# Softmax attention in a hybrid decoder: projections, norms and rotation with tokens on partitions, then transposes

## The chip, the cores and the metric

One core of a Trainium2 chip runs the whole program. The metric is the device time of one launch in microseconds (us). The engines are TensorE (PE), VectorE (DVE), ScalarE (ACT), GpSimd (POOL) and SyncE (SP), which issues most of the DMAs.

## What is computed

Two decoder layers over 256 tokens of width 1024, all in float32. Each layer runs three token mixers on the normed input (softmax attention, gated linear attention, causal pooling), gates and merges them, projects and adds; then a feed-forward part follows, dense in layer 0, the best 2 of 8 experts in layer 1. The change touches the attention branch alone, up to its scores:

```python
def mla_branch(c_q, c_kv, k_rope, positions, g_cq, w_uq, g_ckv, w_ukv, g_qk_q, g_qk_k):
    q = (rms_norm(c_q, g_cq) @ w_uq).reshape(B, S, 8, 96)
    kv = (rms_norm(c_kv, g_ckv) @ w_ukv).reshape(B, S, 8, 64 + 64)
    k_nope, v = kv[..., :64], kv[..., 64:]
    k = concatenate([k_nope, k_rope for every head], axis=-1)      # 64 + 32
    q, k = rms_norm(q, g_qk_q), rms_norm(k, g_qk_k)                # over 96 features
    q, k = (concatenate([z[..., :64], rope(z[..., 64:], positions)], axis=-1) for z in (q, k))
    o = causal_block_attention(q, k, v)
```

`c_q` and `c_kv` have 256 features, `k_rope` 32; all three are columns of one projection of the normed input. `rope` turns the last 32 features of each head by an angle that depends on the token.

## The kernel before

Every engine has its program written out by hand, and semaphores order them. The 1024-wide products run in pieces. A weight block of about 1 MB (256 to 288 columns; one of the names in `LOADS`, such as `cq`, `ckv`, `gq`, `gk`, `oga`, `ogb`, `ua`, `ub`, `g0`) is loaded by SP into one of four ring slots, in the order of `LOADS`. ACT rounds a piece of it (a quarter) to `m_hi` (line 1265), DVE takes the rest `m_lo` (line 1696), and PE multiplies three times: high by high, high by low, low by high (`by_pieces`, line 565). There are four piece buffers, so ACT can round piece p of the next block as soon as PE has used piece p of this one. In `split(L, name, FIRST)` the first three pieces are done, in `split(L, name, LAST)` the fourth; other work of ACT and DVE stands between, in a fixed order.

PSUM: six banks are handed out in turn to the names in `MIX_USES`. A use waits until the use six places ahead of it has been freed. In layer 0 two more uses, `par` and `inv`, stand after the fifth; so `lr` (the second product out of the block `vb`) gets the bank of `va`, which DVE frees by a copy to `gvt` (line 1706) after it has split all of `vb`.

In each layer, from `cq` on, PE does in this order: `cq`, `ckv` with `kr` (the rope part again as a product of its own, 96 columns wide of which 32 count), `gq`, the sums of squares of both latents by a matrix of ones (`sslat`, line 642), `gk`, the query projection `q0` to `q3` (line 528), `oga`, the key projection `k0` to `k3` (line 528) and the value projection `vm0`, `vm1` (line 672), `ogb`, the sums of squares of all queries and keys as 32 products with one column of ones (`ssq`, line 684), the decay gate `z` (line 692), the rotation of the shared rope key by a fixed matrix (`rk`, line 699) and of the queries (`rq0` to `rq3`, line 704), `ua`, the inverse norms of the keys spread over features (`ssk0` to `ssk3`, line 713), `ub`, and then the gate block `g0` with which the scores begin. Queries and keys lie with features on partitions and 256 tokens along the free axis throughout. The plain float32 products (lines 528, 672, 684, 692, 704, 713) issue two matmul instructions each; a transpose issues one.

ACT squares and copies each bank (lines 1327 to 1381) and takes the roots. DVE inverts the latent roots in a 128x512 tile (line 1653), scales the latents (line 1733), copies the values (line 1754), turns the queries (lines 1784 and 1787; POOL multiplies by the cosine, line 1163) and multiplies the keys by their inverse norms (line 1819). Between them DVE and ACT do the decay gate: DVE line 1777, ACT exponential and logarithm (lines 1376 and 1378), DVE lines 1792 and 1793. `tables()` (lines 1628 to 1648) makes sines and cosines once, in layer 0.

## Time and profile before

| | |
|---|---|
| median of 3 runs | 1252.97 us (1252.05 to 1253.17) |
| span of the profiled execution | 1251.2 us |
| PE / DVE / ACT / POOL busy | 94% / 68% / 54% / 7% |
| layer 0, from the start of `cq` to the start of `g0` | 41.3 to 129.5 us |
| layer 1, the same stretch | 515.9 to 604.1 us |
| experts, about | 790 us to the end |

The profiled execution has no time of its own beside its span, which leaves out what lies before the first and after the last instruction: the median stands 1.8 us above it. PE is "busy" from the start of a matmul to its modelled end, and these overlap; what a group of matmuls costs PE is read from the start of one group to the start of the next, and the chain of work gives exactly this.

### The profile page before, as it was taken

Reading aid. Unit: us, or ns where it says so; the run is one execution under the profiler, and the core shown is the slowest. Engines: PE = TensorE matmul, PEld = TensorE weight load, DVE = VectorE, ACT = ScalarE, POOL = GpSimd, SP = SyncE. Lnnn points to the kernel's source line nnn. Section 1 sums busy time; section 2 is a strip of 40 time slices with the busy share of each in tenths; the row PEclk is TensorE's granted clock in tenths of the full one; section 3 lists DMA queues with packets and bytes.
Section 4 is the critical chain, followed back from the end, with each engine's and each line's share of the span. In section 5 each row is a group of like instructions: output and inputs, shape, how many; then the busy total and the mean of one; then the engine's idle time right before and its main releaser. Section 6 shows DMA issues by size and latency. Waiting matters only on the chain.

```text
span 1251.2 us, 17893 instructions
## 1 busy us (share of the span) xinstructions
PE 1171.3 (94%) x6973; PEld 999.6 (80%) x6973; DVE 849.2 (68%) x1090; ACT 680.6 (54%) x922; POOL 88.7 (7%) x149
## 2 busy tenths in 40 slices
PE   3999899988999998999989988799999999999997
PEld 3978777877999998987867776787878888787885
DVE  3366877685545546445877686488888888888786
ACT  3464564544434434464464545376666666676664
POOL 5001412000000000001332000000000000000000
PEclk9998999998999999998989998799999999999999
DMA  6432343537537534242234447189989898988983
GB/s 195 161 104 102 107 139 132 168 121 266 186 124 247 185 134 160 93 136 101 80 123 148 165 135 269 53 306 332 306 297 324 288 341 288 337 302 306 316 303 121
DMA packets 146852, 250.17 MB, mean 200 GB/s; under 512 B 4318, under 2 KB 107860, under 8 KB 146772
## 3 DMA queue, kind: packets, MB, share of 16 engines
q1 hardware_dynamic: 144944, 246.82, 58.0%
q10 hardware_dynamic: 1828, 2.23, 0.6%
q8 instruction: 57, 0.93, 0.3%
q14 instruction: 23, 0.19, 0.1%
HBM read 247.98 MB, written 1.05 MB: 199 GB/s over the span
## 4 chain that ended last, share of the span: by engine, by line
PE 80%; DVE 10%; ACT 4%; issue 3%; POOL 1%; DMA 0%; ACTq 0%; DVEq 0%; POOLq 0%
PE PS L565 23%; PE PS L1047 9%; PE PS L1048 9%; PE PS L1049 9%; PE PS L910 5%; PE PS L912 5%; PE PS L911 5%; DVE m_lo L1696 3%; PE PS L1008 3%; PE PS L528 2%; ACT w_hi L339 2%; DVE w_lo L347 2%; PE PS L684 1%; PE PS L1019 1%; PE PS L591 1%
## 5 line engine op out<-in xcount | busy, mean ns | idle before, releaser
L347 DVE TENSOR_TENSOR w_lo<-ring,w_hi 128x1536 fp32r<-128x1536 f32 (+1 forms) x240 | 388.1, 1623 | 153.2 <-ACT w_hi L339 151.9
L339 ACT ACTIVATE w_hi<-ring 128x1536 fp32r<-128x1536 f32 (+1 forms) x240 | 329.3, 1378 | 160.3 <-PE PS L912 86.0
L1696 DVE TENSOR_TENSOR m_lo<-ring,m_hi 128x512 fp32r<-128x512 f32 (+2 forms) x256 | 185.8, 755 | 102.7 <-ACT m_hi L1265 101.3
L1265 ACT ACTIVATE m_hi<-ring 128x512 fp32r<-128x512 f32 (+2 forms) x256 | 157.6, 630 | 160.6 <-PE PS L565 158.8
L1047 PE MATMUL PS<-w_hi,hTe_hi 128*96 128x384 f32 (+1 forms) x512 | 169.9, 332 | 7.2 <-DVE w_lo L347 5.9
L1048 PE MATMUL PS<-w_hi,hTe_lo 128*96 128x384 f32 (+1 forms) x512 | 165.2, 323 | 0.0
L1049 PE MATMUL PS<-w_lo,hTe_hi 128*96 128x384 f32 (+1 forms) x512 | 165.0, 322 | 0.0
L565 PE MATMUL PS<-m_hi,h_hi 128*128 128x512 f32 (+1 forms) x288 | 108.3, 376 | 5.4 <-DVE gvt L1706 4.2
L565 PE MATMUL PS<-m_hi,h_lo 128*128 128x512 f32 (+1 forms) x288 | 103.3, 359 | 0.0
L565 PE MATMUL PS<-m_lo,h_hi 128*128 128x512 f32 (+1 forms) x288 | 103.0, 358 | 0.0
L910 PE MATMUL PS<-h_hi,w_hi 128*128 128x256 f32 x352 | 100.7, 286 | 0.7 <-DVE h_lo L1678 0.7
L912 PE MATMUL PS<-h_hi,w_lo 128*128 128x256 f32 x352 | 100.5, 286 | 0.0
L911 PE MATMUL PS<-h_lo,w_hi 128*128 128x256 f32 x352 | 100.5, 286 | 0.0
L1047 PEld LDWEIGHTS PS<-w_hi,hTe_hi 128*96 128x96 f32 x512 | 82.6, 161 | 17.8 <-issue 12.0
L1048 PEld LDWEIGHTS PS<-w_hi,hTe_lo 128*96 128x96 f32 x512 | 82.8, 162 | 7.3 <-issue 1.9
L1049 PEld LDWEIGHTS PS<-w_lo,hTe_hi 128*96 128x96 f32 x512 | 82.8, 162 | 5.0
L1047 PE MATMUL PS<-w_hi,hdT_hi 128*96 128x512 f32 x176 | 70.5, 400 | 0.9 <-issue 0.9
L910 PEld LDWEIGHTS PS<-h_hi,w_hi 128*128 128x128 f32 x352 | 68.6, 195 | 1.3 <-issue 1.1
L1048 PE MATMUL PS<-w_hi,hdT_lo 128*96 128x512 f32 x176 | 69.4, 394 | 0.0
L1049 PE MATMUL PS<-w_lo,hdT_hi 128*96 128x512 f32 x176 | 69.2, 393 | 0.0
L911 PEld LDWEIGHTS PS<-h_lo,w_hi 128*128 128x128 f32 x352 | 68.6, 195 | 0.2
L912 PEld LDWEIGHTS PS<-h_hi,w_lo 128*128 128x128 f32 x352 | 68.5, 195 | 0.0
(307 smaller groups left out, 2105.1 us busy)
## 6 DMA issues: line engine op xcount, KB each, us to landing
ring<-in_w_in_dram SPq DMA_DIRECT2D x40, 1024.0 KB, 5.1
ring<-in_w_exp_gate_dram SPq DMA_DIRECT2D x24, 1536.0 KB, 8.0
ring<-in_w_exp_up_dram SPq DMA_DIRECT2D x24, 1536.0 KB, 8.5
ring<-in_w_exp_down_dram SPq DMA_DIRECT2D x24, 1536.0 KB, 7.2
ring<-in_w_branch_dram SPq DMA_DIRECT2D x12, 1024.0 KB, 5.0
ring<-in_w_ffn_gate_dram SPq DMA_DIRECT2D x6, 1536.0 KB, 7.2
ring<-in_w_ffn_up_dram SPq DMA_DIRECT2D x6, 1536.0 KB, 7.1
ring<-in_w_ffn_down_dram SPq DMA_DIRECT2D x6, 1536.0 KB, 6.3
```

Of the source, the lines that this page charges most:

```text
L339: act.activation(w_hi[:, b, 0:words], ring[:, i % NSLOT, w0:w0 + words], ACT.Copy)\
L347: dve.tensor_tensor(w_lo[:, b, 0:words], ring[:, (j // 2) % NSLOT, w0:w0 + words], w_hi[:, b, 0:words].bitcast(F32), SUB).then_inc(sem(f"l ...
L565: mm = pe.matmul(dst, l, r, start=(kt == 0 and x == 0 and y == 0), stop=(kt == total - 1 and y == 2), skip_group_check=True)
L910: pe.matmul(dst, whi, xhi, start=start, stop=False, skip_group_check=True)
L911: pe.matmul(dst, whi, xlo, start=False, stop=False, skip_group_check=True)
L912: return pe.matmul(dst, wlo, xhi, start=False, stop=stop, skip_group_check=True)
L1008: mm = pe.matmul(PS[:, 4 + b, i * CAP:(i + 1) * CAP], htok[:, a, (4 * c + i) * P:(4 * c + i + 1) * P], psel[:, a, e, :], start=(a == 0), s ...
L1047: pe.matmul(dst, xhi, whi, start=start, stop=False)
L1048: pe.matmul(dst, xlo, whi, start=False, stop=False)
L1049: return pe.matmul(dst, xhi, wlo, start=False, stop=stop)
L1265: act.activation(hi, raw, ACT.Copy).then_inc(sem("m_hi_ready"), 1)
L1696: dve.tensor_tensor(lo, raw, hi.bitcast(F32), SUB).then_inc(sem("m_lo_ready"), 1)
```

## The change

Tokens lie on partitions for the attention projections. `cq` and `ckv` are computed by token block; `ckv` gives latent and rope key in one product of 288 columns. ACT takes the latents' sums of squares with an accumulator, DVE inverts four columns; both scale the latents, PE transposes them (`lt0`, `lt1`), and the gains are applied on the way out. Queries and keys with values come in four banks each (`QUADS`: token block, half of the heads). Their sums of squares are DVE reductions. The queries are turned and the keys scaled with tokens on partitions, and PE transposes both (`tq`, `tk`). Rope gains are multiplied into the sine and cosine tables (`rope_factors`, layer 0). Gone are `sslat`, `kr`, `vm`, `ssq`, `rk`, `rq`, `ssk`, `inv` and POOL's cosine products. Six small DMAs are added on SP's queue, one from ACT's queue is gone.

```diff
-MIX_USES = (["hm00", "hm01", "va", "hm10", "hm11", "vb", "lr", "cq", "ckv", "kr", "gq", "sslat", "gk"]
-            + [f"q{i}" for i in range(4)] + ["oga"] + [f"k{i}" for i in range(4)] + ["vm0", "vm1", "ogb", "ssq", "z", "rk"]
-            + [f"rq{i}" for i in range(4)] + ["ua"] + [f"ssk{i}" for i in range(4)] + ["ub"]
+QUADS = [f"{a}{hf}" for a in range(TT) for hf in range(2)]
+MIX_USES = (["hm00", "hm01", "va", "hm10", "hm11", "vb", "lr", "cq", "ckv0", "ckv1", "gq", "lt0", "lt1", "gk"]
+            + [f"q{x}" for x in QUADS] + ["oga"] + [f"kv{x}" for x in QUADS] + ["ogb", "z"]
+            + [f"tq{x}" for x in QUADS] + ["ua"] + [f"tk{x}" for x in QUADS] + ["ub"]
...
-USES[5:5] = [(-1, "par"), (-1, "inv")]
+USES[5:5] = [(-1, "par")]
@@ SP @@
+                if i == 2:
+                    for a in range(TT):
+                        sp.dma_start(posi[:, a:a + 1], A["positions"][:, a * P:(a + 1) * P].rearrange("b p -> p b"))\
+                          .then_inc(sem("pos_in"), 16)
+                    for x, g in enumerate(("g_qk_q", "g_qk_k")):
+                        for L in range(DEPTH):
+                            sp.dma_start(grope[:, x, L, :], A[g][L:L + 1, NOPE:QK].broadcast_to([P, ROPE]))\
+                              .then_inc(sem("grope_in"), 16)
@@ PE @@
+                by_pieces(L, "cq", [by_tokens(L, "cq")])
+                groups = []
+                for a in range(TT):
+                    bank, full = begin(L, f"ckv{a}")
+                    groups.append((full, [(bank[:, 0:RANK + ROPE], 0, RANK + ROPE, a)]))
+                by_pieces(L, "ckv", groups)
                 pair(L, "gq")
...
+                    bank, full = begin(L, f"lt{g}")
+                    for x in (("cq",), ("ckv0", "ckv1"))[g]:
+                        evacuated(L, x)
                     for i in range(KR):
-                        mm = pe.matmul(bank[:, g * T:(g + 1) * T], ones[:, :], sq[:, g * KR + i, :],
-                                       start=(i == 0), stop=(i == KR - 1))
-                mm.then_inc(full, 1)
+                        for a in range(TT):
+                            mm = pe.transpose(bank[:, i * T + a * P:i * T + (a + 1) * P],
+                                              latn[:, a, (g * KR + i) * P:(g * KR + i + 1) * P], ident[:, :])
+                    mm.then_inc(full, 1)
...
+                def from_latent(g, name, cols, w):
+
+                    for x in QUADS:
+                        a, hf = int(x[0]), int(x[1])
+                        bank, full = begin(L, f"{name}{x}")
+                        for i in range(KR):
+                            mm = pe.matmul(bank[:, 0:cols], latT[:, g * KR + i, a * P:(a + 1) * P],
+                                           w[:, i, hf * cols:(hf + 1) * cols], start=(i == 0), stop=(i == KR - 1))
+                        mm.then_inc(full, 1)
...
+                def heads(name, src, ready):
+
+                    for x in QUADS:
+                        a, hf = int(x[0]), int(x[1])
+                        bank, full = begin(L, f"{name}{x}")
+                        pe.wait_ge(sem(ready), L + 1)
+                        for i in range(4):
+                            mm = pe.transpose(bank[0:QK, i * P:(i + 1) * P], src[:, a, 4 * hf + i, :], ident[:, :])
+                        mm.then_inc(full, 1)
+
+                heads("tq", qt, "q_turned")
...
+                heads("tk", kt_, "k_scaled")
@@ ACT @@
+                split(L, "ckv", FIRST)
+                bank, _ = full(L, "cq")
+                for a in range(TT):
+                    act.activation(latsq[:, a, :], bank[:, a * RANK:(a + 1) * RANK], ACT.Square, accum_out=rl[:, a:a + 1])
+                split(L, "ckv", LAST)
+                split(L, "gq", FIRST)
+                for a in range(TT):
+                    bank, _ = full(L, f"ckv{a}")
+                    act.activation(latsq[:, 2 + a, :], bank[:, 0:RANK], ACT.Square, accum_out=rl[:, 2 + a:3 + a])\
+                       .then_inc(sem("latent_squares"), 1)
+                act.wait_ge(sem("latent_squares"), 2 * L + 2)
+                act.activation(rl[:, :], rl[:, :], ACT.Sqrt, bias=eps[:, 0:1], scale=1.0 / RANK).then_inc(sem("latent_roots"), 1)
+                for a in range(TT):
+                    bank, _ = full(L, f"ckv{a}")
+                    act.activation(krt[:, 1, a, :], bank[:, RANK:RANK + ROPE], ACT.Square, accum_out=sskr[:, a:a + 1])
+                    act.activation(krt[:, 0, a, :], bank[:, RANK:RANK + ROPE], ACT.Copy).then_inc(sem("kr_in"), 1)
+                act.wait_ge(sem("latent_inverse"), L + 1)
+                for a in range(TT):
+                    bank, free = full(L, f"ckv{a}")
+                    act.activation(latn[:, a, RANK:2 * RANK], bank[:, 0:RANK], ACT.Copy, scale=rl[:, 2 + a:3 + a]).then_inc(free, 1)
                 split(L, "gq", LAST)
+                split(L, "gk", FIRST)
+                bank, free = full(L, "lt0")
+                for i in range(KR):
+                    ins = act.activation(latT[:, i, :], bank[:, i * T:(i + 1) * T], ACT.Copy, scale=pcol("g_cq", L * KR + i))
+                ins.then_inc(free, 1)
+                split(L, "gk", LAST)
...
+                for x in QUADS:
+                    a, hf = int(x[0]), int(x[1])
+                    bank, _ = full(L, f"kv{x}")
+                    if hf == 0:
+                        act.wait_ge(sem("q_sums"), 2 * L + a + 1)
+                    kv = bank.rearrange("p (h c) -> p h c", h=4)
+                    n = 4 * NOPE
+                    act.activation(sqs[a][:, hf * n:(hf + 1) * n].rearrange("p (h c) -> p h c", h=4), kv[:, :, 0:NOPE], ACT.Square)
+                    act.activation(vt[:, a, hf * 4 * DV:(hf + 1) * 4 * DV].rearrange("p (h c) -> p h c", h=4), kv[:, :, NOPE:], ACT.Copy)\
+                       .then_inc(sem("kv_read"), 1)
+                act.activation(rq16[:, :], rq16[:, :], ACT.Sqrt, bias=eps[:, 1:2])
+                act.wait_ge(sem("k_sums"), L + 1)
+                act.activation(rk16[:, :], rk16[:, :], ACT.Sqrt, bias=eps[:, 0:1], scale=1.0 / QK).then_inc(sem("qk_roots"), 1)
                 split(L, "ua", FIRST)
                 out_gate(1)
                 split(L, "ua", LAST)
+                if L == 0:
+                    act.wait_ge(sem("gains_ready"), 1)
+                for x in QUADS:
+                    a, hf = int(x[0]), int(x[1])
+                    bank, free = full(L, f"tq{x}")
+                    act.activation(q[:, 4 * hf:4 * hf + 4, a * P:(a + 1) * P], bank[0:QK, :].rearrange("p (h t) -> p h t", h=4),
+                                   ACT.Copy, scale=pcol("g_qk_q", L, QK)).then_inc(free, 1)
 
                 act.wait_ge(sem("z_abs"), L + 1)
@@ DVE @@
+            def rope_factors():
+                dve.wait_ge(sem("rope_tables"), 1)
+                dve.wait_ge(sem("grope_in"), 16 * 2 * DEPTH)
+                cos, sin = (cs[:, i, :].rearrange("p (a j) -> p a j", a=TT) for i in range(2))
+                for L in range(DEPTH):
+                    for x in range(2):
+                        g = grope[:, x, L, :].rearrange("p (s j) -> p s j", s=2)
+                        by_cos, by_sin = (ropes[:, L, x, i, :, :].rearrange("p a (s j) -> p a s j", s=2) for i in range(2))
+                        for s in range(2):
+                            gs, other = (g[:, i, :].unsqueeze(1).broadcast_to([P, TT, HALF]) for i in (s, 1 - s))
+                            dve.tensor_tensor(by_cos[:, :, s, :], cos, gs, MUL)
+                            ins = dve.scalar_tensor_tensor(by_sin[:, :, s, :], sin, 1.0 if s else -1.0, other, MUL, MUL)
+                step(ins)
             def latent_inverse(L):
+                dve.wait_ge(sem("latent_roots"), L + 1)
+                dve.reciprocal(rl[:, :], rl[:, :]).then_inc(sem("latent_inverse"), 1)
+                dve.wait_ge(sem("latent_inverse"), L + 1)
+                bank, free = full(L, "cq")
+                for a in range(TT):
+                    ins = dve.tensor_scalar(latn[:, a, 0:RANK], bank[:, a * RANK:(a + 1) * RANK], rl[:, a:a + 1], None, MUL)
+                ins.then_inc(free, 1)
+            def turn_rope(x, tmp, by_cos, by_sin, last):
+                for s in range(2):
+                    ins = dve.tensor_tensor(tmp[..., s * HALF:(s + 1) * HALF], x[..., (1 - s) * HALF:(2 - s) * HALF],
+                                            by_sin[..., s * HALF:(s + 1) * HALF], MUL)
+                step(ins)
+                step(dve.tensor_tensor(x, x, by_cos, MUL))
+                last(dve.tensor_tensor(x, x, tmp, ADD))
...
+                split(L, "ckv"), split(L, "gq", FIRST)
+                latent_inverse(L)
+                split(L, "gq", LAST)
                 split(L, "gk", FIRST)
+                bank, free = full(L, "lt1")
+                for i in range(KR):
+                    ins = dve.tensor_scalar(latT[:, KR + i, :], bank[:, i * T:(i + 1) * T], pcol("g_ckv", L * KR + i), None, MUL)
+                ins.then_inc(free, 1)
...
                 split(L, "ogb", FIRST)
+                for a in range(TT):
+                    freed(L, f"q{a}1")
+                    dve.tensor_reduce(rq16[:, a * H:(a + 1) * H], sqs[a].rearrange("p (h c) -> p h c", h=H), AX.X, ADD)\
+                       .then_inc(sem("q_sums"), 1)
                 out_gate(0)
                 split(L, "ogb", LAST)
+                if L == 0:
+                    rope_factors()
+                by_cos, by_sin = (ropes[:, L, 1, i, :, :] for i in range(2))
+                dve.wait_ge(sem("kr_in"), 2 * L + 2)
+                turn_rope(krt[:, 0, :, :], krt[:, 1, :, :], by_cos, by_sin, step)
+                by_cos, by_sin = (ropes[:, L, 0, i, :, :].unsqueeze(2).broadcast_to([P, TT, H, ROPE]) for i in range(2))
+                turn_rope(qt[:, :, :, NOPE:QK], qtmp, by_cos, by_sin, lambda ins: ins.then_inc(sem("q_turned"), 1))
                 for a in range(TT):
+                    dve.wait_ge(sem("kv_read"), 4 * L + 2 * a + 2)
+                    step(dve.tensor_reduce(rk16[:, a * H:(a + 1) * H], sqs[a][:, 0:H * NOPE].rearrange("p (h c) -> p h c", h=H),
+                                           AX.X, ADD))
+                dve.tensor_tensor(rk16.rearrange("p (a h) -> p a h", a=TT), rk16.rearrange("p (a h) -> p a h", a=TT),
+                                  sskr.unsqueeze(2).broadcast_to([P, TT, H]), ADD).then_inc(sem("k_sums"), 1)
                 split(L, "ua", FIRST)
+                dve.wait_ge(sem("qk_roots"), L + 1)
+                step(dve.reciprocal(rqs[:, :], rq16[:, :]))
+                step(dve.reciprocal(rk16[:, :], rk16[:, :]))
+                for x in QUADS:
+                    a, hf = int(x[0]), int(x[1])
+                    bank, free = full(L, f"kv{x}")
+                    rk = rk16[:, a * H + 4 * hf:a * H + 4 * hf + 4].unsqueeze(2).broadcast_to([P, 4, NOPE])
+                    dve.tensor_tensor(kt_[:, a, 4 * hf:4 * hf + 4, 0:NOPE],
+                                      bank.rearrange("p (h c) -> p h c", h=4)[:, :, 0:NOPE], rk, MUL).then_inc(free, 1)
+                for a in range(TT):
+                    rk = rk16[:, a * H:(a + 1) * H].unsqueeze(2).broadcast_to([P, H, ROPE])
+                    ins = dve.tensor_tensor(kt_[:, a, :, NOPE:QK], krt[:, 0, a, :].unsqueeze(1).broadcast_to([P, H, ROPE]), rk, MUL)
+                ins.then_inc(sem("k_scaled"), 1)
                 out_gate(1)
                 split(L, "ua", LAST)
...
-                turned(2), turned(3)
-                split(L, "ub")
-                dve.wait_ge(sem("krope_read"), 2 * L + 2)
-                for i in range(4):
-                    bank, free = full(L, f"ssk{i}")
-                    x = k[:, 2 * i:2 * i + 2, :]
-                    dve.tensor_tensor(x, x, two(bank[0:QK, :]), MUL).then_inc(free, 1)
+                split(L, "ub", FIRST)
+                for x in QUADS:
+                    a, hf = int(x[0]), int(x[1])
+                    bank, free = full(L, f"tk{x}")
+                    dve.tensor_scalar(k[:, 4 * hf:4 * hf + 4, a * P:(a + 1) * P], bank[0:QK, :].rearrange("p (h t) -> p h t", h=4),
+                                      pcol("g_qk_k", L, QK), None, MUL).then_inc(free, 1)
+                split(L, "ub", LAST)
```

## Rows read from the trace of the kernel before

**Rows 1.** The page, busy time of each engine over the span.
```profile
PE 1171.3 (94%) x6973; PEld 999.6 (80%) x6973; DVE 849.2 (68%) x1090; ACT 680.6 (54%) x922; POOL 88.7 (7%) x149
```

**Rows 2.** Busy time by stretch: start:end, length, each engine, granted clock, DMA.
```profile
31.16:41.28 10.12, 10.12 (x72) 9.29 (x73) 2.58 (x4) 1.90 (x3) 0.00 (x0) 0.83 0.64 214
41.28:129.53 88.25, 88.25 (x601) 76.92 (x599) 52.12 (x88) 46.93 (x71) 5.73 (x4) 0.94 0.36 117
507.31:515.89 8.58, 8.58 (x74) 8.03 (x73) 4.79 (x8) 2.69 (x5) 0.00 (x0) 1.00 0.39 124
515.89:604.13 88.24, 88.24 (x600) 77.07 (x599) 45.47 (x66) 45.30 (x69) 5.80 (x4) 0.94 0.36 117
...
103.30:113.50 10.20, 10.20 (x29) 6.21 (x29) 5.13 (x10) 2.62 (x5) 2.39 (x2) 0.50 0.13 50
151.30:154.50 3.20, 0.38 (x6) 0.14 (x2) 2.96 (x10) 2.63 (x10) 2.95 (x5) 1.00 0.67 251
154.50:161.30 6.80, 6.35 (x20) 5.16 (x21) 6.49 (x15) 3.22 (x9) 5.52 (x7) 0.50 0.21 50
```

**Rows 3.** The chain of work in layer 0: start, length, engine and line.
```profile
21.32 0.54 PE PS L538 x4
...
27.82 2.63 DVE m_lo L1696 x4
30.45 0.61 DVE gvt L1706
...
31.16 30.34 PE PS L565 x240
61.50 1.73 PE PS L642 x8
63.22 5.75 PE PS L565 x48
68.97 6.91 PE PS L528 x32
...
81.63 7.05 PE PS L528 x32
88.68 3.63 PE PS L672 x8
...
98.06 8.57 PE PS L684 x64
...
108.63 6.05 PE PS L704 x8
...
120.44 3.49 PE PS L713 x32
...
137.43 0.43 DVE small L1833
```

**Rows 4.** Groups of DVE in layer 0, `cq` to `g0`, shapes apart.
```profile
L1653 DVE RECIPROCAL rt<-rt 128x512 f32<-128x512 f32 x1 | 3.4, 3353 | 1.1 <-ACT rt L1247 1.1
L1787 DVE TENSOR_TENSOR qk<-qk,th 32x512 f32<-32x512 f32 x4 | 3.2, 806 | 0.1
...
L1819 DVE TENSOR_TENSOR qk<-qk,PS 96x512 f32<-96x512 f32 x4 | 2.5, 679 | 0.0
L1777 DVE SCALAR_TENSOR_TENSOR scr<-scr 128x512 f32<-128x512 f32 x1 | 1.7, 1687 | 0.0
```

**Rows 5.** ACT in order of time, the decay gate of layer 0.
```profile
113.23 1.28 ACT L1378 ACT_TABLE_LOAD   x1
114.52 0.63 ACT L1378 ACTIVATE scr<-scr 128x512 f32<-128x512 f32 x1
```

**Rows 6.** DMA issues up to 140 us: engine, size, us to landing.
```profile
scr<-in_positions_dram ACTq DMA_DIRECT2D x1, 32.0 KB, 6.0
...
wr<-in_w_router_dram ACTq DMA_DIRECT2D x1, 32.0 KB, 9.5
```

**Rows 7.** Waits of SP's DMA queue: waited for, total, times, longest.
```profile
SPq L425 <- PE PS L616: 19.8, 1, 19.8
```

More of the change, by code:

```diff
@@ L252, in hybrid_trunk @@
         rk16 = small[:, 32:48]
+        rl, sskr = small[:, 28:32], small[:, 61:63]
         warmth = small[:, 60:61]
@@ L616, in parameters @@
                 pe.transpose(bank[:, 0:NPAR], ring[0:NPAR, NSLOT - 1, 0:P], ident[0:NPAR, 0:NPAR]).then_inc(full, 1)
-                bank, full = begin(-1, "inv")
-                pe.matmul(bank[0:QK, 0:1], invr[:, :], one1[:, :], start=True, stop=True).then_inc(full, 1)
             def mixer(L):
@@ L678, in mixer @@
-                evacuated(L, "q3")
-                evacuated(L, "k3")
-                for c, src in enumerate((sq, sk)):
-                    for a in range(TT):
-                        for h in range(H):
-                            x = c * TT * H + a * H + h
-                            mm = pe.matmul(bank[:, x:x + 1], src[0:QK, h, a * P:(a + 1) * P], ones[0:QK, 0:1],
-                                           start=True, stop=True)
-                mm.then_inc(full, 1)
+                evacuated(L, "lt1")
@@ L1240, in two @@
                 return ap.rearrange("p (a t) -> p a t", a=2)
-            def latent_root(L):
-                bank, free = full(L, "sslat")
-                if L:
-                    act.wait_ge(sem("latn_ready"), 4 * L)
-                act.activation(rt[:, :, :], two(bank), ACT.Sqrt, bias=eps[:, 0:1], scale=1.0 / RANK).then_inc(free, 1)
             warm = [0]
@@ L1316, in mixer @@
                     act.activation(par[:, :], bank[:, 0:NPAR], ACT.Copy).then_inc(free, 1)
-                    bank, free = full(-1, "inv")
-                    act.activation(invc[NOPE:QK, :], bank[NOPE:QK, 0:1], ACT.Copy).then_inc(free, 1)
+                    freed(-1, "par")
+                    c = PCOL["g_qk_q"]
+                    act.activation(par[NOPE:QK, c:c + 2 * DEPTH], ones[NOPE:QK, 0:2 * DEPTH], ACT.Copy).then_inc(sem("gains_ready"), 1)
                 split(L, "vb")
```

217 lines of the change are left out of this document (49 added, 168 removed).

## The prediction, made before the changed kernel ran

> **What bounds the kernel now.** I read the page first: PE is busy 94% of the span, DVE 68%, ACT 54% [rows 1]. Then I asked for busy time by stretch where the change acts, from the start of `cq` to the start of `g0`: 88.25 us in layer 0 and 88.24 us in layer 1, and in both PE has no idle time at all [rows 2]. DVE is busy 52.1 and 45.5 us there, ACT 46.9 and 45.3, so both have slack, but not so much that PE could shrink without end. Last I read the chain of work, which stays on PE from 31 us until the scores [rows 3]. What PE no longer does in this stretch should thus come off the time, less the waits that a faster PE runs into. The stretch is also at half clock in one place: 0.50, the lower level (1.2 GHz), from 103.3 to 113.5 us, after PE had done some 5 us of products with a single column [rows 2, 3].
>
> **PE's work in the stretch, rebuilt.** Prices per matmul instruction come from the chain [rows 3]. A float32r product of 256 columns is 5.75/48 = 0.12 us. A float32 one of 256 columns is 6.91/32 = 0.216 us, hence 0.324 for 384 and 0.43 for 512. A transpose is 0.54/4 = 0.135 us with the group's end in it; I take 0.12.
> - `cq`, `gq`, `gk`, `oga`, `ogb`, `ua`, `ub`, as before: 7 x 5.75 = 40.25.
> - `ckv` and `kr`: 72 instructions become 48 of 288 columns. No row has that width; at one column per cycle and the same fixed part 0.135 each, 6.45 (before 72 x 0.12 = 8.6). Bounds: 5.75 if width were free, 8.6 if nothing were won.
> - `sslat` (1.73) becomes 8 transposes, 1.0.
> - Queries: 32 x 256 columns become 16 x 384, 5.2 (before 6.91).
> - Keys and values: 7.05 + 3.63 = 10.7 become 16 x 512, 6.9.
> - `ssq`, 8.57, and `rk`, 0.4: nothing.
> - `z`: 1.6, what is left of the gap between the `ssq` and `rq` rows.
> - `rq`: 6.05 (at half clock; 8 x 0.43 = 3.4 at full) becomes 16 transposes, 1.9.
> - `ssk`: 3.49 becomes 16 transposes, 1.9.
>
> Sum 65.2 us, say 65.5 for the changes between kinds, against 88.25: 22.8 us less per layer. Nearly half is `ssq`, with the clock that it costs `rq`.
>
> **The clock.** Without one-column products, what can still pull it down is waiting or a run of transposes. The rows show a fall after a stretch in which PE was busy for 0.38 of 3.20 us: 0.50 for the following 6.8 us [rows 2]. The longest wait that I find below is 1.1 us; I take no new fall. The Trainium skill ("TensorE: Matmul & The Clock Gate", Part 4, PE-mode transpose) says that transposes do not count as activity for the clock gate in the way matmuls do. No transposes here stand alone for more than 1 us in a busy part, so no row settles it; that outcome is a rival below, priced from rows.
>
> **The start of layer 0.** `lr` takes the bank of `va` and waits for the copy to `gvt`, which ends at 31.1 us behind four low parts [rows 3]. With `inv` gone, `lr` gets the bank of `hm01`, long free, and PE begins `vb` when the first low part is there: 27.82 + 0.69 = 28.5 instead of 31.16, 2.65 us earlier. After the long wait `vb` ran at clock 0.83 and took 10.12 us; in layer 1, at 1.00, 8.58 [rows 2]. With a wait of under 2 us I expect full clock: 1.5 more. Together 4.2; bounds 2.65 and 4.2.
>
> **DVE and ACT.** DVE loses the 128x512 reciprocal 3.35, four scalings of latents (4 x 0.48), two copies of values (2 x 0.69), eight operations of turning (4 x 0.69 + 3.2), the key scaling 2.5 and three small ones of 0.42: about 16.3 us [rows 4]. It gains, at about 1 ns per column and 0.15 fixed (0.43 for a reduction over 256 columns [rows 3], 0.68 for 512): latents 1.9, query sums 2 x 0.95, turning of rope key and queries 0.8 + 2.4, key sums 2 x 0.69 + 0.2, key scaling 1.8 + 0.8, copies out of `tk` 2.5: 13.7. So DVE gets 43 us of work in 68 in layer 1; in layer 0 `tables` shrinks from 256 to 32 columns and 16 small operations of about 0.2 (3.2 us) come in. ACT loses about as much as it gains, plus one table load of 1.28 [rows 5], since a root now stands between the two tanh. Neither becomes the bound by sum; order decides. POOL's part was off the path.
>
> **The new waits**, with 0 at the end of the `kv` products:
> - ACT reads the banks as they fill and is done at 0.9. In layer 0 DVE splits the end of `ogb` at -3.6, makes rope factors until -0.4 and turns until 2.3. Key sums 3.9, root 4.2. ACT's three pieces of `ua` 5.9, DVE's 6.6, inverses 7.1; then four scalings of 0.45 free the `kv` banks at 7.5, 8.0, 8.4, 8.9; rope keys 9.7; the second output gate 10.4 frees `ogb`'s bank.
> - PE ends `ogb` at 5.8 and `z` at 7.3. `tq` needs the `kv` banks: wait 0.3, end 9.3. `ua` needs the bank of `ogb`: wait 1.1. In layer 1 there are no rope factors, and both together are about 0.9.
> - The decay gate has lost the turnings that filled its waits. DVE adds and takes absolute values until 13.7 (2 x 0.44 + 1.69 behind the last piece of `ua` at 11.1), ACT takes exponential, table load and logarithm (0.63 + 1.28 + 0.63 [rows 5]) to 16.3, DVE 1.67 + 0.43 to 18.4, and only then splits `ub`: first piece 19.1. PE has done `ua` and `tk` at 18.0: wait 1.1, and 0.1 at the fourth piece, which stands behind the `tk` copies.
> - Latents: roots, rope key and scaling stand before ACT's last piece of `gq`. From the end of `ckv`: squares 0.7, root 1.0, rope key 2.1, scaling 2.9, high 3.55, low 4.3; PE wants it at 4.3: 0 to 0.3.
>
> Sum 2.6 us in layer 0, 2.1 in layer 1. Behind `g0` DVE, ACT and POOL stand to PE as before, so scores, pooling and all later stages move ahead unchanged; their loads start when ring slots are freed, hence earlier too.
>
> **The sum.** 4.2 + (22.8 - 2.6) + (22.8 - 2.1) = 45.1. The profiled span of 1251.2 becomes 1206.1; the median stands 1.8 above it: 1252.97 - 45.1 = 1207.9, say 1208. All waits covered: 1203. Turning or key scaling at twice my price: 2 to 4 us more per layer, one for one in layer 0, since `k_sums` stands ahead of ACT's `ua`.
>
> **Rivals.**
> - *Late chain.* Sums, roots, inverses and scalings now run between DVE and ACT with PE behind them. For: `kv` banks stay held for 8 us after the products. Against: 43 us of DVE work in 68. With 3 to 6 us per layer beyond my waits: 1214 to 1220. Chance 0.14.
> - *Clock.* If transposes are no activity, `tq` with its waits, from 7.3 to 10.5, and `tk` with its wait, 16.2 to 19.1, look like the idle 3.2 us that brought 6.8 us at 0.50 [rows 2]. Each costs up to 3.4 us; one per layer 1215, both 1222. That is what the skill's sentence on transposes would give. Against: the waits alone are short, 1.1 us at most. Chance 0.16.
> - *No gain.* PE's free time is all eaten by DVE's order: it would need 22 us of new waits per layer with DVE idle meanwhile. 1252, chance 0.02.
> - *Slower, through SP's queue.* Two position loads in pieces of 4 bytes and four gain loads in rows of 128 bytes, 768 pieces in all, stand ahead of the `ckv` load. That load waits for the parameters until about 26.7 us anyway (19.8 us of waiting [rows 7]) and is wanted at 38. Bounds [rows 6]: the router load, 1024 pieces, landed in 9.5 us, so 7 us; the old position load, 32 rows, took 6.0 us, and at 0.19 each 768 take 144 us, `ckv` comes 120 us late, and the time is 1330. It loses from 12 us in the queue on, and is slower than before from some 57 us on. The router row is much the nearer. Chance 0.02.
>
> **Chances.** The forecast has 0.66 (its own range 1203 to 1212), and with the late chain and the clock the change is faster in 0.96. The range 1203 to 1219 holds the forecast, nearly all of the late chain and most of the clock. A measurement of this kernel tells 0.2% (2.5 us) from no change; only the no-gain case lies within it, only the queue above it.
>
> **What would show it.** The stretch `cq` to `g0` at 68.1 us in layer 0 and 67.6 in layer 1; clock 1.00 in it; `vb` of layer 0 from 28.5 on, in 8.6 us; no line like `ssq`; waits of PE ahead of `tq`, `ua` and `ub` of about 1 us each. A stretch over 71 us, a clock of 0.5 near `tq` or `tk`, or a wait of PE behind `ckv`'s load would prove me wrong, each in its own way.

## The result, and the profile after

The changed kernel took 1201.92 us (median of 4 runs, 1200.91 to 1202.44), the kernel before in the same session 1253.07 us (4 runs, 1252.05 to 1254.45): ratio 0.959, 95% interval 0.9577 to 0.9602, 51 us less. The forecast of 1208.0 was 6.1 us too high, and the time lies 1.1 us below the low end of the range. The span of the profiled execution is 1200.6 us, 1.3 below the median.

The page of the changed kernel, busy time of each engine:

```profile
PE 1122.1 (93%) x6695; PEld 959.9 (80%) x6695; DVE 836.8 (70%) x1118; ACT 670.8 (56%) x950; POOL 73.7 (6%) x119
```

PE has lost 49 us of busy time, DVE 12, ACT 10, POOL 15 (against [rows 1]). Busy time by stretch, with the columns of [rows 2]: `vb` of layer 0, `cq` to `g0` of layer 0, the same two of layer 1, and the place behind `g0` where the clock fell before:

```profile
28.71:37.34 8.63, 8.63 (x73) 8.08 (x74) 4.94 (x8) 2.63 (x5) 0.00 (x0) 1.00 1.07 362
37.34:102.08 64.74, 64.50 (x462) 57.77 (x461) 45.44 (x110) 41.98 (x85) 0.00 (x0) 1.00 0.47 146
479.99:488.58 8.59, 8.59 (x75) 8.04 (x74) 4.80 (x8) 2.70 (x5) 0.00 (x0) 1.00 0.42 125
488.58:553.33 64.75, 64.51 (x463) 57.77 (x461) 39.74 (x72) 40.54 (x83) 0.00 (x0) 1.00 0.47 146
124.00:127.30 3.30, 0.28 (x6) 0.09 (x2) 3.05 (x10) 2.74 (x9) 3.05 (x5) 1.00 0.66 255
127.30:134.20 6.90, 6.62 (x21) 5.34 (x22) 6.59 (x14) 3.33 (x10) 5.27 (x7) 0.51 0.25 62
```

The second column is the length. The stretch is 64.74 and 64.75 us long where it was 88.25 and 88.24, its clock 1.00 instead of 0.94, and PE idles 0.24 us in it. `g0` begins at 102.08 instead of 129.53: 27.45 earlier, of which 3.94 were won by the start of `cq` (37.34 for 41.28) and 23.51 in the stretch. Layer 1 gives 23.49. Together 50.94, against 50.6 between the two spans, so behind `g0` the time is the same to 0.3 us. The last two rows show one place of it: PE is busy for 0.28 us of 3.3, then runs 6.9 us at half clock, as in [rows 2].

The chain of work of the changed kernel in layer 0, with the columns of [rows 3]:

```profile
27.84 0.74 DVE m_lo L1700
28.71 26.70 PE PS L574 x216
...
62.03 5.16 PE PS L662 x16
...
72.94 6.87 PE PS L662 x16
...
88.08 0.61 DVE ys L1751
88.73 6.01 PE PS L574 x48
94.75 1.75 PE PS L691 x16
```

The long rows of [rows 3] at L684, L704 and L713 (8.57, 6.05, 3.49) have no successor but L691, the transposes of queries and keys. Products of queries and of keys with values are the rows at L662 (5.16 for 6.91, 6.87 for 7.05 and 3.63). The chain leaves PE once between 29 and 107 us, from 84.13 to 88.73, ahead of `ua`: ACT and DVE split the third piece of `ua`, which waited for PE to be done with `ogb`'s third piece, then DVE does the inverses, the key scaling and the output gate `ys`. PE works beside most of this; what it lost there is in the waits below.

### The profile page after: what moved, and what is told of

It reads as the page before. It is cut to its first block, busy times and chain, and to the rows that moved or that the text cites. A ratio compares the mean times of both kernels' runs of the same rounds, so it can differ in the third digit from the quotient of the medians.

```text
span 1200.6 us, 17376 instructions
## 1 busy us (share of the span) xinstructions
PE 1122.1 (93%) x6695; PEld 959.9 (80%) x6695; DVE 836.8 (70%) x1118; ACT 670.8 (56%) x950; POOL 73.7 (6%) x119
## 4 chain that ended last, share of the span: by engine, by line
PE 82%; DVE 9%; ACT 4%; issue 3%; POOL 1%; DMA 0%; ACTq 0%; DVEq 0%; POOLq 0%
PE PS L574 25%; PE PS L1028 9%; PE PS L1029 9%; PE PS L1030 9%; PE PS L891 5%; PE PS L892 5%; PE PS L893 5%; PE PS L989 3%; PE PS L662 2%; DVE m_lo L1700 2%; ACT w_hi L345 2%; DVE w_lo L353 2%; PE PS L1000 1%; PE PS L600 1%; PE PS L757 1%
## 5 line engine op out<-in xcount | busy, mean ns | idle before, releaser
L574 PE MATMUL PS<-m_hi,h_hi 128*128 128x512 f32 (+2 forms) x352 | 126.5, 360 | 3.3 <-DVE m_lo L1700 2.7
L574 PE MATMUL PS<-m_hi,h_lo 128*128 128x512 f32 (+2 forms) x352 | 121.2, 344 | 0.0
L574 PE MATMUL PS<-m_lo,h_hi 128*128 128x512 f32 (+2 forms) x352 | 121.2, 344 | 0.0
L574 PEld LDWEIGHTS PS<-m_hi,h_hi 128*128 128x128 f32 x352 | 67.2, 191 | 14.3 <-issue 3.0
L574 PEld LDWEIGHTS PS<-m_hi,h_lo 128*128 128x128 f32 x352 | 67.2, 191 | 7.9 <-issue 0.5
L574 PEld LDWEIGHTS PS<-m_lo,h_hi 128*128 128x128 f32 x352 | 67.0, 190 | 8.0
```

The costliest lines, as they stand in the source:

```text
L574: mm = pe.matmul(dst, l, r, start=(kt == 0 and x == 0 and y == 0), stop=(kt == total - 1 and y == 2), skip_group_check=True)
```

## The experiments

All kernels were timed beside the kernel before on the same chip, whose median was 1253.69 us for the first four, 1253.06 for the next four and 1254.16 for the last three. Those named "before plus" start from the kernel before, the others from the changed one.

### Before plus: `inv` put into the bank of `par`

```diff
-USES[5:5] = [(-1, "par"), (-1, "inv")]
+USES[5:5] = [(-1, "par")]
-                bank, full = begin(-1, "inv")
-                pe.matmul(bank[0:QK, 0:1], invr[:, :], one1[:, :], start=True, stop=True).then_inc(full, 1)
+                pe.matmul(bank[0:QK, 64:65], invr[:, :], one1[:, :], start=True, stop=True).then_inc(full, 1)
```

> The kernel before, with one thing of the change: the product for the inverse frequencies goes into the bank of the parameters, so that lr no longer gets the bank of va. Theory (the bank order alone made the start of layer 0 slow): PE begins vb at 28.5 to 28.7 us instead of 31.16, the product runs at clock 1.00 in 8.6 us, and all later stages move ahead by 3.9 us: 1249. Rival (the start was won by something else of the change, fewer steps on POOL or the moved position load): no change, 1253.

Measured: 1250.67 us (10 runs, 1248.07 to 1254.09), ratio 0.9978, interval 0.9961 to 0.9994. Its chain at the start, and busy time of `vb`:

```profile
28.00 0.74 DVE m_lo L1694
28.87 30.15 PE PS L565 x240
```

```profile
28.87:38.80 9.93, 9.93 (x72) 9.29 (x73) 4.94 (x8) 2.63 (x5) 0.00 (x0) 0.85 0.94 320
```

PE starts `vb` right behind the first low part, 2.29 us before the 31.16 of [rows 3]; the copy `gvt` is out of the chain. The part of the wait is shown. The clock part is not: PE idled for 2.02 us here and 2.1 in the changed kernel, but here `vb` ran at 0.85 (0.83 in [rows 2], after 4.25 us), in the changed kernel at 1.00. So of the 3.94 us at the start of the changed kernel 2.45 are the earlier start of `vb` (28.71 for 31.16) and 1.49 its shorter run (8.63 for 10.12), and in this trace the shorter wait alone did not bring the second part.

Two things limit this. The trace is of one execution, 1252.94 us, above the median of its ten; three of the ten took 1248.1 to 1248.5, where the theory (1249) would put them, at a mean granted clock of 0.969 to 0.970 over the whole program for 0.966 here; at which places their clock fell less is not known. On the other side, all nine traces of the changed kernel and of its variants below have `vb` at 1.00 from 29 to 37 us behind a wait of 2.1 us. So something else of the change may take part; what, these runs do not show.

### Before plus: POOL's cosine products left out

This kernel leaves out the cosine part of the queries' rotation; POOL writes one column instead.

```diff
-                    pool.tensor_tensor(x, x, cos, MUL).then_inc(sem("cos_done"), 1)
+                    pool.memset(dum[:, 4 * L + i:4 * L + i + 1], 0.0).then_inc(sem("cos_done"), 1)
```

> The kernel before, without POOL's products of the queries with the cosine (a one-column memset of POOL gives the signal instead, so the queries' rope part is left unmultiplied). Theory (POOL's products with two SBUF inputs slow the two gate steps of DVE that also have two SBUF inputs): lines 1777 and 1792 take 0.69 us each instead of 1.69 and 1.67, but PE has no wait to lose in this stretch, so the time stays within 0.1% of 1253. Rival (the gate steps are slow for another reason, such as their own operands): 1.69 and 1.67 stay.

Measured: 1253.39 us (10 runs), ratio 1.0006, interval 0.9991 to 1.0022: the time is unchanged, as the theory had it. The two decay-gate steps of DVE by the timeline (start, length, engine, line), first in the kernel before, then here, and between them POOL in the kernel before:

```profile
110.86 1.69 DVE L1777 SCALAR_TENSOR_TENSOR scr<-scr 128x512 f32<-128x512 f32 x1
115.95 1.67 DVE L1792 SCALAR_TENSOR_TENSOR scr<-scr 128x512 f32<-128x512 f32 x1
```

```profile
110.74 1.26 POOL L1163 TENSOR_TENSOR qk<-qk,rows 32x512 f32<-32x512 f32 x1 [88.99 <-PE PS L704]
112.37 1.30 POOL L1163 TENSOR_TENSOR qk<-qk,rows 32x512 f32<-32x512 f32 x1 [0.37 <-PE PS L704]
113.91 3.17 POOL L1163 TENSOR_TENSOR qk<-qk,rows 32x512 f32<-32x512 f32 x2 [0.23 <-PE PS L704]
```

```profile
110.82 0.69 DVE L1778 SCALAR_TENSOR_TENSOR scr<-scr 128x512 f32<-128x512 f32 x1
114.42 0.69 DVE L1793 SCALAR_TENSOR_TENSOR scr<-scr 128x512 f32<-128x512 f32 x1
```

The instruction costs 0.69 us; the 1.69 and 1.67 that I carried into the changed kernel were POOL's doing. The rows also fit one way in which this can happen: POOL's products end at 110.74 + 1.26 = 112.00 and 113.91 + 3.17 = 117.08, and DVE's steps end at 112.55 and 117.62, 0.55 and 0.54 after. It looks as if DVE stood still until POOL was done and then did its work. The Trainium skill ("SBUF — State Buffer", section "SBUF: two separate sides") says just that: a VectorE operation with two inputs in SBUF and a GpSimd operation that reads SBUF share a port pair as an exclusive lock, whoever starts first has it for the whole instruction. The trace agrees for the two steps shown.

### Before plus: two products for all sums of squares

Of the 32 one-column products two of 16 columns are left, so all heads and tokens get the sums of one head's first 128 tokens; the other sums are left out.

```diff
-                    for a in range(TT):
-                        for h in range(H):
-                            x = c * TT * H + a * H + h
-                            mm = pe.matmul(bank[:, x:x + 1], src[0:QK, h, a * P:(a + 1) * P], ones[0:QK, 0:1],
-                                           start=True, stop=True)
+                    mm = pe.matmul(bank[:, c * 16:c * 16 + 16], src[0:QK, 0, 0:P], ones[0:QK, 0:16], start=True, stop=True)
```

> The kernel before, with two products in place of the 32 one-column ones (the sums of squares of the other heads and tokens are left out). Theory (the one-column products cost their own time and pull the clock down for rq): 8.3 us less for the products, 2.6 less because rq runs at clock 1.00, and about 1 us of new wait at ub: 10 us per layer, 1233. Rival (the clock falls at that place anyway, because of z or the short products behind it): 8.3 us per layer less the wait, 1238 or 1239, and a clock of 0.50 near rq.

Measured: 1237.3 us (4 runs, 1235.03 to 1238.0), ratio 0.9864, interval 0.9842 to 0.9887: 16.4 us less, not the 20 of the theory (1233); the time is nearer to the rival's 1238, but the clock is not as the rival had it. The chain in layer 0 of this kernel, and the clock:

```profile
105.39 0.89 DVE scr L1770 x2
...
106.33 7.51 PE PS L565 x48
113.83 3.49 PE PS L709 x32
117.33 11.24 PE PS L565 x72
```

```profile
107.60:111.00 3.40, 3.40 (x19) 3.40 (x19) 3.23 (x6) 3.35 (x4) 0.00 (x0) 0.56 0.00 0
111.00:117.00 6.00, 6.00 (x55) 6.00 (x54) 5.80 (x10) 3.36 (x6) 0.00 (x0) 1.00 0.01 3
```

The half clock at `rq` is gone, with `z` and the short products still in place, so it did come with the one-column products. But PE, 8 us ahead of before, now waits 2.7 us for DVE's read of `z` (line 1770), whose bank `ua` takes, and the clock falls behind that wait for 3.4 us (0.56) and stretches `ua` from 5.75 to 7.5. By stages, from start to start: the sums -8.2, `z`, `rk` and `rq` without the half clock -2.8, the wait +2.7, `ua` in the new fall +1.2, together -7.1 from `ssq` to `ub`. `ub` started at 117.33 for 123.93, 6.6 us earlier, since this execution came 0.5 us later to `ssq`; in layer 1 it started 13.8 us earlier (584.71 for 598.54), 7.2 more. Taking the sums off TensorE alone gives part of its price back; the changed kernel keeps more of it, since there `ua` waits less than half a microsecond.

### The query transposes issued six times

```diff
-                        for i in range(4):
+                        for i in [0, 1, 2, 3] * (6 if name == "tq" else 1):
```

> The changed kernel with each transpose of the queries done six times over, 96 in a row instead of 16, so that nearly 10 us pass with transposes alone. Theory (transposes keep the clock up as products do): clock 1.00 throughout, 80 x 0.107 = 8.6 us more per layer less the 0.7 us of waits it covers, 1201.9 + 16 = 1218. Rival (for the clock a transpose is as good as idle): the clock falls to 0.50 inside the run of transposes, each then takes 0.21 us, ua behind them begins slow too, and the time is 1225 to 1235.

Measured: 1221.83 us (4 runs, 1217.09 to 1224.62), ratio 0.9734, interval 0.9705 to 0.9764; the theory said 1218, the rival 1225 to 1235. Busy time over the 96 transposes and over `ua` behind them:

```profile
86.48:96.92 10.44, 10.44 (x97) 10.44 (x97) 4.31 (x10) 2.73 (x5) 0.00 (x0) 1.00 0.35 112
96.92:103.00 6.08, 6.08 (x54) 6.08 (x52) 2.55 (x5) 4.83 (x8) 0.00 (x0) 1.00 0.01 3
```

Ten microseconds of nothing but transposes, and the clock stays at 1.00 in them and behind them. 10.44/96 = 0.109 us each, where I took 0.12. The rival by which transposes bring the clock down is dead, at least for these float32 ones of 128 columns. Of the 19.9 us more than the changed kernel, 2 x 8.2 are in these stages (16.28 us from the start of the transposes to the end of `ua`, where the changed kernel takes 8.05). The profiled execution has falls of the clock elsewhere that the changed kernel's trace lacks (0.50 near 241 and 702 us), which I can't tie to the transposes; they may be the rest, and the wide scatter.

### POOL given work beside the decay gate

Five idle POOL products of 32 x 384, once DVE has read `z`.

```diff
+                _, _, free, n = use(L, "z")
+                pool.wait_ge(free, n + 1)
+                for i in range(5):
+                    step(pool.tensor_tensor(dum[:, :], dum[:, :], dum[:, :], MUL))
```

> The changed kernel with idle work for POOL: five products of 32x384 with two SBUF inputs as soon as DVE has freed the bank of z, where POOL's cosine products ran before. Theory (beside such work DVE's gate steps take 1.7 us instead of 0.69): the gate is 2 us later, the first low part of ub comes at about 97.4 us instead of 95.4, PE waits 1.1 to 1.3 us for it in each layer, and the time is 2 to 2.5 us above the changed kernel's 1201.9: 1204. Rival (the gate steps are fast for another reason): both stay at 0.69 and the time at 1202.

Measured: 1203.53 us (5 runs, 1200.49 to 1206.22), ratio 0.9607, interval 0.959 to 0.9624; span 1201.1, 0.5 above the changed kernel. The median is 1.6 us above it, but the two intervals overlap, so the reading rests on the trace. DVE in the changed kernel, then DVE and POOL here:

```profile
93.56 0.69 DVE L1799 SCALAR_TENSOR_TENSOR scr<-scr 128x512 f32<-128x512 f32 x1 [2.64 <-ACT scr L1358]
94.29 0.43 DVE L1800 TENSOR_SCALAR cum<-scr 128x512 f32<-128x512 f32 x1
```

```profile
90.06 0.69 DVE L1801 SCALAR_TENSOR_TENSOR scr<-scr 128x512 f32<-128x512 f32 x1
93.40 1.28 DVE L1804 SCALAR_TENSOR_TENSOR scr<-scr 128x512 f32<-128x512 f32 x1 [2.64 <-ACT scr L1363]
94.72 0.93 DVE L1805 TENSOR_SCALAR cum<-scr 128x512 f32<-128x512 f32 x1
90.11 5.25 POOL L1135 TENSOR_TENSOR dum<-dum 32x384 f32<-32x384 f32 x5 [73.48 <-DVE scr L1798]
```

The first step started 0.05 us before POOL and was spared; the second and third lost 1.1 us together. Measured from the start of the second step, `ub`'s low parts could start 1.1 us later (the third step ends at 95.65 for 94.72), but PE waited 0.19 only, and the stretch grew by 0.5 us. The stretch of layer 1 grew by the same 0.5. So this POOL work costs about half a microsecond per layer, half of what I had expected: the chain behind the decay gate had 0.7 us of slack in the changed kernel, none in my forecast. POOL worked beside the gate only in part here, and the two steps took 1.1 us more together, not 2.

### DVE delayed ahead of the key sums: 2 and 6 idle instructions

Both kernels differ in the number `n` alone, 1.1 and 3.4 us of DVE time.

```diff
+                for i in range(n):
+                    step(dve.tensor_tensor(dum[:, :], dum[:, :], dum[:, :], MUL))
                 for a in range(TT):
                     dve.wait_ge(sem("kv_read"), 4 * L + 2 * a + 2)
```

> The changed kernel with two idle DVE products of 384 columns, 1.1 us together, ahead of the key sums in each layer. Theory (0.6 us of slack, since ACT waits for PE at its third piece of ua): PE loses 0.5 us per layer, 1203. Rival (the chain of sums, roots and scalings has no slack): 1.1 us per layer, 1204. Second rival (much slack): nothing.

> The changed kernel with six idle DVE products of 384 columns, 3.4 us together, ahead of the key sums in each layer. Theory (0.6 us of slack and then one for one, the later gate included in the same delay): 2.8 us per layer, 1207.5. Rival (as my prediction put it for layer 0, one for one from the start): 3.4 per layer, 1208.7. Second rival (the 0.85 us that ub has over is spent as well, so PE loses less): below 1206.

Measured: 1204.11 us (5 runs; ratio 0.9614, 0.9601 to 0.9627) and 1206.83 us (5 runs; 0.9623, 0.961 to 0.9636). Waits of PE in layer 0 of the first kernel, then in layer 0 and layer 1 of the second (engine, line, waited for, total, times, longest):

```profile
PE PS L692 <- DVE big L1787: 0.5, 1, 0.5
PE PS L575 <- DVE ys L1752: 0.3, 1, 0.3
```

```profile
PE PS L692 <- DVE big L1787: 2.9, 1, 2.9
...
PE PS L692 <- DVE big L1787: 1.1, 1, 1.1
```

The end of `ua` moved by 0.67 us in layer 0 and by nothing in layer 1 for 1.1 us of delay. For 3.4 us of delay it moved by 5.2 and 1.3. From that, DVE's chain has about 0.45 us of slack in layer 0 and 2.1 in layer 1; the difference, 1.65, is about what the rope factors take in layer 0 (1.7). The medians alone would not tell this: 1204.11 is the first rival's number (1204), though not one for one by the trace, and 1206.83 lies between the theory (1207.5) and the second rival (below 1206). In layer 0 the larger delay cost more than itself, and the clock says why:

```profile
80.00:87.80 7.80, 5.68 (x43) 5.08 (x41) 6.60 (x13) 4.11 (x7) 0.00 (x0) 0.99 0.76 267
87.80:94.60 6.80, 6.02 (x29) 5.87 (x30) 5.10 (x12) 5.59 (x9) 0.00 (x0) 0.51 0.30 74
```

After a wait of 2.9 us PE ran 6.8 us at half clock. In layer 1 the wait was 1.1 us, and the clock stayed. So the "late chain" rival was near in layer 0 alone: 3.4 us more of DVE work ahead of the key sums, and it begins there, with the clock rival behind it, while layer 1 loses 1.3 us and the whole time, 1206.83, is still below my forecast.

### The pooling held: until `pt3`, until `g2`, and in two parts

Behind `g0` the old wait stands unchanged (the last two rows of busy time in the result). In the changed kernel POOL's big pooling additions start at 116.78 while DVE writes the low parts of `g2`:

```profile
115.11 6.59 DVE L1700 TENSOR_TENSOR m_lo<-ring,m_hi 128x512 fp32r<-128x512 f32 x4 [0.29 <-ACT m_hi L1222]
...
127.24 0.85 PE L720 MATMUL PS<-ident,Pr 128*128 128x128 f32 x3 [3.02 <-DVE Pr L1854]
```

Four low parts take 6.59 us where they take 2.63 alone ([rows 3], 27.82), and PE then waits for the softmax. POOL slows only some of DVE's operations: the low parts have both inputs in SBUF, while the two row sums of the next softmax step (line 1842), in which DVE reduces one tile beside the third addition, take 0.74 us with POOL and without. The first kernel holds POOL until `pt3` is full:

```diff
                 decayed(1), decayed(2)
+                _, f, _, n = use(L, "pt3")
+                pool.wait_ge(f, n + 1)
```

> The changed kernel with POOL's causal pooling held back until the fourth head's probabilities are transposed, some 12 us later. Theory (pooling on POOL slows DVE's low parts of g2 from 2.5 to 6.6 us, which makes PE wait 3.3 us for the probabilities and then run at clock 0.50 for 6.9 us): the wait and the fall go, up to 6.7 us per layer come in, and POOL slows another part of DVE by 1 to 4 us: 1190 to 1198. Rival (the slow stretch only moves with POOL's work, with its wait and its fall): 1200 to 1205.

Measured: 1204.4 us (5 runs; ratio 0.9615, 0.9602 to 0.9628), no gain, as the rival had it. DVE's low parts of `g2` and `g3`, and the waits of PE:

```profile
114.41 3.46 DVE L1702 TENSOR_TENSOR m_lo<-ring,m_hi 128x512 fp32r<-128x512 f32 x4 [0.29 <-ACT m_hi L1224]
...
123.88 5.63 DVE L1702 TENSOR_TENSOR m_lo<-ring,m_hi 128x512 fp32r<-128x512 f32 x4
```

```profile
123.99 0.52 PE L720 MATMUL PS<-ident,Pr 128*128 128x128 f32 x3 [0.39 <-DVE Pr L1856]
136.97 0.88 PE L720 MATMUL PS<-ident,Pr 128*128 128x128 f32 x3 [4.87 <-DVE Pr L1856]
```

The slow stretch went with POOL from one weight block to the next: the 3.02 is 0.39, and a new one of 4.87 stands behind `g3`. The next kernel lets POOL go between the two blocks, the third holds the twelve small pooling instructions as well until the low parts of `g3` are written:

```diff
                 decayed(1), decayed(2)
+                pool.wait_ge(sem("m_lo_ready"), piece_no(L, "g2", PIECES - 1) + 1)
...
+                pool.wait_ge(sem("m_lo_ready"), piece_no(L, "g3", PIECES - 1) + 1)
                 for g, w in enumerate(WINDOWS):
```

> The changed kernel, with POOL's pooling held until DVE has written all four low parts of g2 (about 118 us in layer 0; in the changed kernel it runs 116.8 to 132.9, in the kernel that held it until pt3 was full 124.6 to 140). Theory: the big pooling additions (6.5 us) slow DVE's low parts alone, so they must fall between those of g2 and those of g3: g2's stay at 3.4 us, the wait of PE for the third and fourth softmax (3.3 us) and the 6.9 us at half clock behind it go, g3's low parts start at 123.2, beside the last 1 to 2 us of the additions, and take 3 to 4 us: no wait over 1 us there. 3.3 + 3.4 us less per layer, 1188 to 1191 us. Rival (only moves, as with the later hold): g3's low parts are slowed from 3.1 to 5 us or more by the rest, and the wait comes behind g3: 1199 to 1204.

> As the run before, with the twelve small pooling instructions (16 to 256 columns) held as well until DVE has written all low parts of g3. Theory: no pooling beside the low parts of g3 but the end of the additions; 1188 to 1191 us, within 1 us of the kernel with one hold, since the small instructions slow low parts by half a microsecond at most (3.1 instead of 2.6 beside them). Rival: the small ones matter too, and this kernel is 3 us or more faster than the one with one hold; or pooling ends too late for the product that reads it, and this one is slower by the wait.

> The changed kernel as it is, beside the two kernels with holds on the same chip: 1202 us, ratio 0.959 to the kernel before, with the wait of 3.3 us for the softmax and 6.9 us at half clock behind it in each layer.

Measured on one chip: one hold 1197.38 us (1195.61 to 1200.45, ratio 0.9562, 0.9542 to 0.9583), two holds 1199.71 (1196.17 to 1202.41, ratio 0.9563, 0.9543 to 0.9583), the changed kernel 1201.5 (1200.63 to 1202.31, ratio 0.9585, 0.9569 to 0.9601), 4 runs each. With one hold:

```profile
126.04 3.21 DVE L1701 TENSOR_TENSOR m_lo<-ring,m_hi 128x512 fp32r<-128x512 f32 x4
```

```profile
125.24 0.52 PE L720 MATMUL PS<-ident,Pr 128*128 128x128 f32 x3 [1.32 <-DVE Pr L1855]
...
136.09 0.52 PE L720 MATMUL PS<-ident,Pr 128*128 128x128 f32 x3 [1.82 <-DVE Pr L1855]
```

Low parts are 3.5 and 3.2 us now, as expected, but the wait did not vanish. It fell apart into 1.32 and 1.82: the additions now run beside DVE's softmax steps (a step of the decay levels, line 1818, takes 1.18 us for 0.42) and delay those a little. PE's waits for the softmax between 100 and 152 us (line 720) add up to 4.3 us in the changed kernel, to 5.7 with POOL held until `pt3`, 4.1 with one hold and 3.7 with two: they are cut up, hardly less. The half clock, 6.9 us before, is there for about 3.4 us with one hold. That is not surely the hold's doing: behind the unchanged wait of 3.0 us it also lasted only about 3.4 us in layer 0 of the kernel with two idle instructions (0.50 from 128.5 to 131.5, back at 0.95 behind it) and in layer 1 of the one with POOL beside the decay gate.

The product that follows the head section began at 147.53 instead of 149.47 in layer 0, and at 594.49 instead of 600.73 in layer 1, in the fastest of the four runs (1195.61). Against the changed kernel the medians differ by 4.1 us, a third of the 12 that I had hoped for. All four runs with one hold were faster than all four of the changed kernel, but the intervals of the two ratios overlap by 0.0014, so it is likely faster, not surely. Both theories (1188 to 1191) missed. The second hold shows no gain: its ratio is the same, its runs scatter over 6 us.

## Why the prediction was right or wrong

The direction and the main mechanism held: PE's own work came off, less some waits, SP's queue cost nothing, and what lies behind `g0` kept its length. But the forecast, 1208.0, was 6.1 us too high, and two terms of its sum failed. PE's work in the stretch was put at 65.5 us and measured 63.9, which makes 3.2 us over both layers; the new waits were put at 2.6 and 2.1 us and measured 0.8 in each layer, 3.1 us. It was the work that put the time below the range: the low end, 1203, is the sum with every wait at nothing and PE's work taken as exact, and the measured 1201.92 is below it with 1.6 us of waits still in. The queue did what the nearer row said: the six small loads held SP's queue from 6.28 to 13.22 us (6.9, said 7), 4.94 of it for the two position loads, and the `ckv` load went out at about 26.7 us as before.

**The start**: 3.94 us, forecast 4.2. `vb` from 28.71 (said 28.5), in 8.63 us at clock 1.00 (said 8.6). The bank is shown. The clock came out right by luck as far as is known: I expected it from a wait of under 2 us; the wait was 2.1, and the kernel with the bank alone waited 2.02 and ran `vb` at 0.85 in its trace.

**PE's work in the stretch** was too high. Taking stages from start to start: `ckv` 6.39 (6.45 said), latent transposes 0.79 (1.0), queries 4.87 (5.2), keys and values 6.47 (6.9), `z` 0.72 without its wait (1.6), `tq` 1.74 at the 0.109 of a transpose (1.9), `tk` 1.66 (1.9): 22.6, where I had 25.0. The seven 256-column products with the changes between kinds measured 41.3, where I had 40.25 and 0.3 for the changes. Together 63.9 for my 65.5, 1.6 us per layer. The largest single error is `z`, 0.9 us too much: I read it as a gap between two rows, and that gap held the half clock.

**The waits.** I forecast 2.6 us in layer 0 and 2.1 in layer 1; the weight loads of PE (PEld) show 0.33 ahead of `tq` and 0.49 ahead of `ua`, 0.8 in either layer and none ahead of `ub`:

```profile
86.54 1.70 PEld L691 LDWEIGHTS PS<-ident,big 128*96 128x96 f32 x16 [0.33 <-DVE big L1782]
88.73 0.19 PEld L574 LDWEIGHTS PS<-h_hi,m_hi 128*128 128x128 f32 x1 [0.49 <-DVE ys L1751]
```

The excess, 1.8 and 1.3 us, has three sources. First, I let the 1.69 and 1.67 us of lines 1777 and 1792 stand for the decay-gate steps in a kernel where POOL no longer works beside them, and wrote that "POOL's part was off the path". It was off PE's path, but it slowed DVE: alone each step takes 0.69, so the chain ahead of `ub` is 2.0 us shorter than I had it, and of the 1.2 us of waits at `ub` nothing was left. Giving POOL work there again brought back half a microsecond. Second, the rope factors: sixteen at 0.2 one after another, 3.2 us; they start 0.10 apart while each takes 0.18, as the timeline shows:

```profile
75.85 0.19 DVE L1636 TENSOR_TENSOR ropes<-cs,grope 128x32 f32<-128x32 f32 x1
75.96 0.18 DVE L1637 SCALAR_TENSOR_TENSOR ropes<-cs,grope 128x32 f32<-128x32 f32 x1
```

so 1.7 us for all sixteen, from 75.85 to 77.57. Third, four key scalings in 1.42 instead of 1.8 and two of the rope key in 0.75 instead of 0.8. Key sums were done 2.9 us after the key products instead of 3.9. The two delays measured the slack of this chain: 0.45 us in layer 0, where I had put none, and 2.1 in layer 1.

Layer by layer: 68.1 - 64.74 = 3.4 is 1.6 of work and 1.8 of waits, 67.6 - 64.75 = 2.9 is 1.6 and 1.3. With 0.26 less at the start, 0.3 less behind `g0` and a median 1.3 instead of 1.8 above its span that makes the 6 us. Nearly all errors of size in the stretch went one way, since nearly every unknown price had been rounded up; a range of 5 us below the forecast that counted only the waits ("all waits covered: 1203") left no room for the work being cheaper too.

**The rivals.** Late chain: not here, but 3.4 us more of DVE work brings it in layer 0 (not in layer 1), so its 0.14 was not too much. Clock: transposes do not bring it down, shown by 96 in a row at 1.00; the Trainium skill's sentence on transposes in "TensorE: Matmul & The Clock Gate" (Part 4, PE-mode transpose) is not borne out for this form. Waits do: those of 2.7 and 2.9 us, each made by the edit of its run, were followed by half clock, the one of 1.1 us was not. No gain and the slow queue: neither.

**The share of the one-column products.** I wrote that nearly half was `ssq` with the clock that it costs `rq`. Taken out alone it gave 16.4 us of the 50.9, a third, with new waits eating part of it.

## What to carry to other kernels

A duration read from a trace belongs to what ran beside it. Before a VectorE step is carried into a changed kernel, look at what GpSimd did at that time: where two of them end together, the step's own price is the one of its twins elsewhere. When an operation is removed from an engine "off the path", ask which other engine it slowed and whose bank or buffer it held. A low end of a range that takes only one term at its best is too high if another term was rounded up as well. And work taken off the bounding engine is only kept if the next engine's order has slack at that point; a delay of known length put there measures it in one run.

## What the runs showed that I had not expected

- GpSimd's products and additions can more than double the time of a VectorE operation beside them: 0.69 us became 1.69, four low parts 6.59 for 2.63. The large losses are on operations with both inputs in SBUF, but a short one with a single input went from 0.43 to 0.93 too; row sums lost nothing. Moving POOL's work mostly moved the loss: of three holds one gained 4.1 us by the medians.
- The position loads, 128 pieces of 4 bytes each, take about 2.5 us each to issue: 4.94 us of SP's queue for two (SyncE in order of time, changed kernel).

```profile
6.28 4.94 SPq L479 DMA_DIRECT2D scr<-in_positions_dram  x2
11.26 0.92 SPq L483 DMA_DIRECT2D grope<-in_g_qk_q_dram  x2
```

- The clock of the same stretch differs between kernels for no reason that I found: `vb` at 1.00 behind a wait of 2.1 us in the changed kernel, at 0.85 behind one of 2.02 in the kernel with `inv` moved. Elsewhere too the length of a wait does not decide it: a wait of 1.32 us was followed by 0.50 in the kernel with two holds (125.4 to 128.6 us), while in the kernel with one hold the clock stayed at 1.00 behind the same wait and fell to 0.50 behind the next, of 1.82. What decides it stays open.
